# Feed-forward gate products of pairs 3 to 10 by seven half-size products (a Strassen scheme with weight and token sums) in a transformer stack on one Trainium2 core

## What is computed

```
def swiglu(h, w_gate, w_up, w_down):
    return (jax.nn.silu(h @ w_gate) * (h @ w_up)) @ w_down

h = rms_norm(x, ffn_norm[i])
x = x + swiglu(h, ffn_w_gate[i], ffn_w_up[i], ffn_w_down[i])
```

## Time and profile before

| | |
|---|---|
| median of three runs | 2059.2 us |
| the profiled execution | 2057.88 us, of which the span of instructions is 2055.9 us |
| TensorE, matmuls | busy 2024.0 us of the span (98%) |
| VectorE, ScalarE, GpSimd | busy 44%, 41%, 50% |
| first feed-forward block | pairs 3 to 10 from 258.8 to 432.9 us, the last down matmuls at 552 us |
| second feed-forward block | pairs 3 to 10 from 865.1 to 1039.2 us, the last down matmuls at 1158 us |

### The profile page before, as it was taken

The page is one execution under the profiler, slowest core; times in us unless marked ns, Lnnn a source line. Parts: engine busy times, 40 slices in busy tenths (PEclk is TensorE's granted clock), DMA queues, the critical chain, the costliest instruction groups (busy, mean ns, idle before and its releaser), DMA issues.

```text
span 2055.9 us, 25781 instructions
## 1 busy us (share of the span) xinstructions
PE 2024.0 (98%) x9884; PEld 1654.1 (80%) x9884; DVE 896.8 (44%) x1411; ACT 840.8 (41%) x1341; POOL 1032.9 (50%) x855
## 2 busy tenths in 40 slices
PE   9999999999999999999999999999999999999998
PEld 7888888888877777888888778988887876677787
DVE  3184433322144435334322388778875215443331
ACT  4123222222244443222222377677774325544543
POOL 4455544545532224544545468788885441323242
PEclk9999999999999999999999999999999999999999
DMA  5223233223433312333233334434432321112131
GB/s 169 97 87 113 83 103 103 84 84 97 126 91 93 92 42 82 103 103 102 84 89 101 102 105 123 122 104 114 133 103 62 105 84 62 60 63 81 43 103 62
DMA packets 259365, 193.28 MB, mean 94 GB/s; under 512 B 9459, under 2 KB 247335, under 8 KB 259256
## 3 DMA queue, kind: packets, MB, share of 16 engines
q1 hardware_dynamic: 256188, 190.67, 30.9%
q10 hardware_dynamic: 3068, 1.09, 0.2%
HBM read 189.46 MB, written 2.27 MB: 93 GB/s over the span
## 4 chain that ended last, share of the span: by engine, by line
PE 38%; issue 35%; POOL 21%; DVE 2%; ACT 2%; DMA 1%; POOLq 0%; SPq 0%; ACTq 0%; DVEq 0%
POOL wlo L652 21%; PE bank L2058 11%; PE bank L2060 11%; PE bank L2059 11%; PE bank L2541 1%; PE bank L2537 1%; PE bank L2505 1%; DMA raw<-in_conv_w_in 0%; DVE xc L1668 0%; ACT whi L741 0%; DVE hLo L1971 0%; DMA rows<-cums 0%; PE bank L2519 0%; PE bank L2493 0%; PE bank L2477 0%
## 5 line engine op out<-in xcount | busy, mean ns | idle before, releaser
L652 POOL TENSOR_TENSOR wlo<-raw,whi 128x512 fp32r<-128x512 f32 (+1 forms) x664 | 842.4, 1299 | 942.7 <-ACT whi L741 942.7
L2058 PE MATMUL bank<-hHi,whi 128*128 128x512 f32 (+1 forms) x1392 | 548.4, 394 | 3.8 <-DVE qk L1554 1.5
L2060 PE MATMUL bank<-hHi,wlo 128*128 128x512 f32 (+1 forms) x1392 | 540.7, 388 | 0.0
L2059 PE MATMUL bank<-hLo,whi 128*128 128x512 f32 (+1 forms) x1392 | 540.4, 388 | 0.0
L741 ACT ACTIVATE whi<-raw 128x2048 fp32r<-128x2048 f32 (+1 forms) x167 | 301.8, 1807 | 476.0 <-PE bank L2060 473.0
L2058 PEld LDWEIGHTS bank<-hHi,whi 128*128 128x128 f32 x1392 | 261.4, 188 | 63.2 <-issue 6.6
L2060 PEld LDWEIGHTS bank<-hHi,wlo 128*128 128x128 f32 x1392 | 261.3, 188 | 54.8
L2059 PEld LDWEIGHTS bank<-hLo,whi 128*128 128x128 f32 x1392 | 261.5, 188 | 53.2 <-issue 1.2
L2058 PE MATMUL bank<-whi,hHi 128*128 128x256 f32 (+1 forms) x640 | 219.4, 343 | 2.2 <-POOL wlo L652 1.8
L2060 PE MATMUL bank<-whi,hLo 128*128 128x256 f32 (+1 forms) x640 | 208.5, 326 | 0.0
L2059 PE MATMUL bank<-wlo,hHi 128*128 128x256 f32 (+1 forms) x640 | 208.3, 326 | 0.0
(11 more groups left out here) (387 smaller groups left out, 2930.7 us busy)
## 6 DMA issues: line engine op xcount, KB each, us to landing
raw<-in_ssd_w_in SPq DMA_DIRECT2D x48, 512.0 KB, 4.8
raw<-in_ffn_w_gate SPq DMA_DIRECT2D x44, 512.0 KB, 4.7
raw<-in_ffn_w_up SPq DMA_DIRECT2D x44, 512.0 KB, 4.7
raw<-in_gla_w_in SPq DMA_DIRECT2D x40, 512.0 KB, 4.6
rows<-cums SPq DMA_DIRECT2D x64, 256.0 KB, 5.4
raw<-in_ffn_w_down SPq DMA_DIRECT2D x32, 384.0 KB, 3.6
raw<-in_attn_w_qkv SPq DMA_DIRECT2D x24, 512.0 KB, 4.5
raw<-in_conv_w_in SPq DMA_DIRECT2D x23, 512.0 KB, 4.4
```

Of the source, the lines that this page charges most:

```text
L652: ins = pool.tensor_tensor(wlo[s][:, part], raw[s][:, part], whi[s][:, part].bitcast(F32), ALU.subtract)
L2058: pe.matmul(dst, hi1, hi2, start=first, stop=False)
L2059: pe.matmul(dst, hi1, lo2, start=False, stop=False)
L2060: return pe.matmul(dst, lo1, hi2, start=False, stop=last)
```

## The change

Only the feed-forward blocks change, and in them pairs 3 to 10 (eight of eleven). The gate product of such a pair is no longer one unit. The product of a weight block (1024 rows by 256 columns) and the tokens (1024 by 512) is cut in two by two quarters in the inner dimension and the columns, and inner dimension and tokens, and is made by seven products of half size in every dimension, with sums of weight quarters (`S1` to `S4`) and sums of token quarters (`T1` to `T4`). Each of the seven is 4 inner tiles by 3 matmuls of 128 x 256, 84 matmuls of 256 columns in place of 48 of 512. The up unit stays 48 matmuls of 512, in four parts of 12 (`u0` to `u3`). TensorE goes through eleven parts in the order of `TURNS`; `S2` and `S3` are added on to bank 0 after its contents were copied out (`kept`), `S4` on to bank 1 after bank 1 was read.

- **Buffers.** `whi` and `wlo` become a ring of eight quarters of 128 x 512. ScalarE rounds each quarter (`turn_high`) once TensorE is through with the part eight turns back, GpSimd makes its low part (`turn_low`). Per pair that is 11 roundings and 11 subtractions of 512 in place of 2 of 2048 and 8 of 512.
- **Added, per pair.** VectorE: the four weight sums of the next pair (512 wide, both inputs and the output in SBUF), four additions of 256 wide that put the blocks of the gate tiles together from a bank and a kept copy (`block`), two products with `rstd` in SBUF (`scaled`, in place of the two reads from the bank). ScalarE: three copies of 256 wide out of bank 0 (`kept`).
- **Added, per block.** ScalarE writes the gained input plain (8 copies, after pair 0); VectorE makes the four token sums of it (1024 wide); ScalarE rounds them in four copies of 1024, GpSimd makes their low parts in eight subtractions of 512 (before unit 5 and before the turns of pair 3).
- **Moved.** VectorE no longer writes `aHi` and `aLo` in each pair; it leaves the plain product (`plain`, which lies where `aLo` is). The 22 roundings (`act_high`, ScalarE) and 22 subtractions (`odd_low` GpSimd, `even_lows` VectorE) come in the last pair and where the down product begins, since the sums lie where `aHi` is. The down product's first output tile waits for these.
- **Waits.** Before the first part of pair 3 TensorE waits for the `a_done` of both tiles of pair 2. SyncE loads the next gate unit after the low part of `22` and the sum `S4` of the pair, the next up unit after the low part of `u3`.

The core of the diff:

```diff
+TURNS = ["11", "12", "S2", "S1", "S3", "22", "u0", "S4", "u1", "u2", "u3"]
...
+            def turn_low(j, i, name):
+                pool.wait_ge(*late("q_hi", turned_by(j, i, name)))
+                pool.tensor_tensor(v3(slot(wlo, j, i, name), 4), source(j, i, name), v3(slot(whi, j, i, name), 4).bitcast(F32),
+                                   ALU.subtract).then_inc(L("q_lo"), 1)
...
+                for t in (1, 3, 5):
+                    odd_low(j, t)
+                pool.sem_inc(w_lo, 2 * SEVENS)
+                low(u_down + 1, 0, DOWN)
+                for t in (7, 9, 11, 13, 15):
+                    odd_low(j, t)
+                low(u_down + 2, 1, DOWN)
+                for t in (17, 19, 21):
+                    odd_low(j, t)
...
+                def turn_high(i, name):
+                    r = turn_at(i, name)
+                    if r >= 8:
+                        act.wait_ge(*late("q_mm", QUARTERS * j + r - 7))
+                    else:
+                        act.wait_ge(mm, 2 * (u_up + 2 * FIRST_SEVEN - (r < 4)))
...
+                    act.activation(v3(slot(whi, j, i, name), 4), source(j, i, name), ACT.Copy).then_inc(L("q_hi"), 1)
...
+                def sevens(i):
+                    kept(i, 0, "11")
+                    turn_high(i, "u1")
+                    turn_high(i, "u2")
+                    kept(i, 1, "S2")
+                    turn_high(i, "u3")
+                    kept(i, 2, "S3")
+                    if i == FT // 2 - 1:
+                        for t in range(8):
+                            act_high(t)
+                        gate_silu(i, 0, 1)
+                        turn_down(0)
+                        gate_silu(i, 1, 0)
+                        for t in range(8, 19):
+                            act_high(t)
+                        turn_down(1)
+                        for t in range(19, FT):
+                            act_high(t)
+                        return
...
-                        chain(tt(t32[b][:, :], bank[2 + b][:, :], tile(sil, b), ALU.mult))
-                        chain(tt(t32[b][:, :], t32[b][:, :], rstd[:, :], ALU.mult))
-                        chain(dve.tensor_copy(tile(aHi, 2 * i + b), t32[b][:, :]))
-                        tt(tile(aLo, 2 * i + b), t32[b][:, :], tile(aHi, 2 * i + b).bitcast(F32), ALU.subtract).then_inc(S(f"a_done{j}"), 1)
...
+                def up(i, b, src, n):
+                    dve.wait_ge(S(f"sil_ready{j}"), 2 * i + n + 1 + 1)
+                    chain(tt(plain(j, 2 * i + b), src[:, :], tile(sil, b), ALU.mult))
+                    tt(plain(j, 2 * i + b), plain(j, 2 * i + b), rstd[:, :], ALU.mult).then_inc(S(f"a_done{j}"), 1)
...
+                def sevens(i):
+                    more = i < FT // 2 - 1
+                    block(i, 0, 0, 0, bank[2], "12")
+                    block(i, 1, 1, 2, bank[1], "S1")
+                    block(i, 1, 0, 2, bank[3], "22")
+                    if more:
+                        first_sums(i + 1)
+                    scaled(i, 1, 3)
+                    block(i, 0, 1, 1, bank[1], "S4")
+                    scaled(i, 0, 4)
+                    if more:
+                        last_sums(i + 1)
+                    else:
+                        even_lows((0, 2, 4, 6))
+                    for b in range(2):
+                        dve.wait_ge(*late("q_mm", turned_by(j, i, f"u{2 * b + 1}")))
+                        up(i, b, bank[4 + b], 1 - b)
+                        if not more and b == 0:
+                            even_lows((8, 10, 12))
...
+                def quarter(dst, i, name, moving, first, width, last=True):
+                    pe.wait_ge(*late("q_lo", turned_by(j, i, name)))
+                    hi, lo = slot(whi, j, i, name), slot(wlo, j, i, name)
+                    for n in range(4):
+                        w = slice(P * n, P * (n + 1))
+                        Hi, Lo = moving(n)
+                        to, begin = dst[:, 0:width], first and n == 0
+                        pe.matmul(to, hi[:, w], Hi, start=begin, stop=False, skip_group_check=True)
+                        pe.matmul(to, hi[:, w], Lo, start=False, stop=False, skip_group_check=True)
+                        ins = pe.matmul(to, lo[:, w], Hi, start=False, stop=last and n == 3, skip_group_check=True)
+                    ins.then_inc(L("q_mm"), 1)
...
+                    if again:
+                        pe.wait_ge(*late("kept", 3 * v))
+                    else:
+                        pe.wait_ge(S(f"gs_ready{j}"), 2 * i + 1)
+                        pe.wait_ge(S(f"a_done{j}"), 2 * i + 1)
+                    quarter(bank[0], i, "11", half(0, 0), True, 256)
+                    if again:
+                        pe.wait_ge(*late("c_made", 4 * v))
+                    quarter(bank[2], i, "12", half(1, 0), True, 256)
+                    pe.wait_ge(*late("kept", 3 * v + 1))
+                    quarter(bank[0], i, "S2", summed(i, 2, 0), False, 256)
+                    quarter(bank[1], i, "S1", summed(i, 0, 1), True, 256)
+                    pe.wait_ge(*late("kept", 3 * v + 2))
+                    quarter(bank[0], i, "S3", summed(i, 1, 2), False, 256)
+                    quarter(bank[3], i, "22", summed(i, 3, 3), True, 256)
+                    if again:
+                        pe.wait_ge(S(f"a_done{j}"), 2 * i)
+                    quarter(bank[4], i, "u0", whole(0), True, SEQ, False)
```

## The result

The changed kernel takes 2065.02 us (median of 9 runs, 2062.89 to 2066.57) against 2059.63 for the kernel before (9 runs): a ratio of 1.0028, 95% interval 1.0020 to 1.0036. It is slower by 0.28%. The forecast was 2054.0 us and faster. The profiled execution took 2064.30 us with a span of 2062.6, 6.4 us more than the one before.

A forecast was written before the change was run, and what follows sets the result against it. TensorE, busy 98% of the span, was taken as the bound. Profiled 2057.88 - 13.0 (narrower gate matmuls) + 5.0 + 2.8 (two stalls) = 2052.7, median 1.3 above: 2054.0 us; range for 8 in 10, 2048.0 to 2066.5.

The forecast's parts named there:

- The gain: Gate units in pairs 3 to 10: 84 narrow matmuls replace 48 wide ones, 0.81 us less each, 13.0 us in all.
- Borders with satisfied waits: Rival: each of 176 part borders costs TensorE even when its wait is satisfied; 0.03 us each erases the gain; chance 0.17.
- the copies out of bank 0 kept their margin: Rival: ScalarE's kept copies miss their 0.8 us margin in the pairs; 0.3 us past it costs 4.8 us; chance 0.07 with other late waits.
- Stall 1: Where pair 3 begins, TensorE waits for pair 2's last up tile: 2.5 us a block, 5.0 in all, bounds 1.8 and 2.9.
- stall 2: Where down begins, TensorE waits for GpSimd's low parts of units two and three: 1.4 us a block, bounds 0 and 2.6.
- The rival that I gave 0.10: GpSimd held up by VectorE steps with two SBUF inputs at down start: 6.2 us a block, 2066.4 us; chance 0.10.
- the forecast's own mechanism: Matmul gain less the stalls at pair 3 and down start: 2054.0 us, bounds 2049.8 to 2057.2; chance 0.58.
- The wider range: Whole-kernel time range for 8 in 10: 2048.0 to 2066.5 us.
- the first rival: At down start, GpSimd held up by VectorE steps with two SBUF inputs: 2066.4 us; chance 0.10.

The follow-up runs named there:

- e8_bank_start: Changed kernel with pair 3 waiting for each bank separately and VectorE's even-tile subtractions at down start reading one input from PSUM bank 7: 2046.75 us, 0.9943 of the kernel before.
- e3_start: Changed kernel with TensorE at pair 3 waiting for each bank by itself, not for both up tiles at the first part: 2059.49 us, 1.0005 of the kernel before.
- e1_bank_input: Changed kernel with VectorE's even-tile subtractions at down start taking one input from PSUM bank 7 (values not the product's): 2053.16 us, 0.9973 of the kernel before.
- e7_share: Changed kernel with per-bank waits at pair 3, ScalarE and GpSimd reordered at down start, tiles 19 and 21 moved to VectorE: 2048.86 us, 0.9951 of the kernel before.

## Why the prediction was wrong

**The gain was right.** 13.0 us by the two pitches: the pairs run without a gap at 0.120 and 0.227, and e8_bank_start finds 12.3 us. Borders with satisfied waits cost nothing that shows (0.4 us a block in all, against 0.03 us each in the rival), and the copies out of bank 0 kept their margin (the first of the last pair ended at 411.35, and S2 began at 412.20): both of those rivals fall. By the gap that the Trainium skill gives for isolated matmuls (TensorE: Matmul & The Clock Gate, Back-to-back issue gap) the gain would have been an estimated 19 us; the trace decides against it.

**Stall 1 was nearly right.** 2.5 us forecast, 2.05 measured with 0.07 of a longer first matmul. VectorE's product with `rstd` took 1.03 us, between my 0.69 and 1.40: it began at 259.63, when 0.44 us of a GpSimd step were left (that one's successor began at 260.07 and took 1.73). e3_start takes the stall away and gains 4.7 us, against 5.0 forecast for it.

**The step that failed is the size of stall 2**, 1.4 us a block against 4.6. The chain was the right one and began on time (the first down unit's low part at 423.14, which is 13.8 us after the last pair's start at 430.32 - 20.95, forecast 13.9). What followed was priced at 3.65 to 4.32, 6.8 and again 3.65 to 4.32 us and took 5.30, 8.55 and 5.37: 19.2 against the 14.1 to 15.4 of the bounds. The rival that I gave 0.10, GpSimd held up by VectorE, is what happened; e1_bank_input shows it, with 14.8 us for the same three groups once VectorE reads a bank. Alone the three groups would be 3.65 + 5 x 1.26 + 3.65 = 13.6 us, and 14 VectorE steps with two SBUF inputs lay beside them (eleven tiles, two products with `rstd`, one scaling; the first and the last in part), 0.40 us of GpSimd's time for each. That rival had nine steps at 0.69 us and no half clock, so its 2066.4 lies near the 2065.0 measured by luck, as its errors cancel; its mechanism was right.

I had argued against it from GpSimd's 5.48 with VectorE's steps beside it against 5.45 without. The 5.45 was not without: VectorE's fourth step, with both inputs in SBUF, began at 391.48, and more such steps lay beside other groups of the pairs. A group in the trace of before that had no VectorE step with two SBUF inputs beside it, ahead of the second block, is

```profile
788.99 5.04 POOL L652 TENSOR_TENSOR wlo<-raw,whi 128x512 fp32r<-128x512 f32 x4 [2.19 <-ACT whi L741]
```

1.26 a step, and the group just before it had taken 5.91. One VectorE step with two SBUF inputs in a group already cost GpSimd 0.4 us (5.45 against 5.04), two cost it 0.9 (5.91 in the trace of before, 7.22 against 5 x 1.26 in e1_bank_input, 4.53 against 3.65 in e7_share), and the eleven that e1_bank_input changed, in 20 us, cost it 4.4. So the price is 0.4 to 0.45 us for each such step, and the steps could have been counted.

**The half clock was not in the sum**, a term put at nothing without a reason. It cost 1.6 us at the first pair 3 and 1.7 and 2.9 at the down starts, 6.2 in the profiled execution. In the two feed-forward blocks of these traces, all four gaps of 4.6 us (the changed kernel and e3_start, two blocks each) went with a stretch at the half clock, three of ten gaps of 2.05 to 2.53 us did, and none of the gaps of 1.2 or less. Why three of the ten did and seven did not stays open. Together: stall 2 was 6.4 us too small, the clock 6.2, stall 1 0.8 too large: 2054.0 + 6.4 + 6.2 - 0.8 = 2065.8 against 2065.0.

The bounds of the forecast's own mechanism, 2049.8 to 2057.2, did not hold the time, and it went the other way than forecast. The wider range held it only because it took in the first rival.

## What to carry to other kernels

Before pricing work that goes to two engines at once, find a group of the one that had the other idle for its whole length, and one that had it busy, and count the steps of the other in it: a pair of rows that differ by 0.03 us says nothing if both have company. Where a queue takes over many small steps at a border, follow every unit that is behind them, not only the next: relieving the second showed the third. A wait of some microseconds on TensorE can be dearer than its length, since a stretch at half clock can follow; several waits of 0.2 to 0.8 us in its place cost in these traces only themselves and 0.1 us each for the start.

## What the runs showed of the hardware

- A GpSimd subtraction of 128 x 512 took 1.26 us alone, and 1.71 to 1.74 with VectorE steps with two SBUF inputs beside it throughout; VectorE's own then took 1.4 to 1.7 in place of 0.69. With one input in PSUM, VectorE took 0.62 a step and GpSimd 3.65 / 4 = 0.91 for the narrow ones with no two-input step beside them, and 7.22 / 5 = 1.44 for the wide ones with two. The Trainium skill (SBUF — State Buffer, Who interferes with whom) says that a VectorE instruction with two SBUF inputs contends with a GpSimd one that reads SBUF, and that the second to come fully blocks until the first is through. The trace agrees that either side can lose, but GpSimd lost 0.4 to 0.45 us for each VectorE step and not its full 0.69.
- In the pairs the same contention is present (GpSimd's steps beside a two-input step were 1.74) and cost nothing, as GpSimd was ahead: in the last pair its low parts of S2 and S1 ended at 405.26 and 406.96, and TensorE began them at 412.20 and 413.64.
- At the half clock (TensorE granted 1.2 GHz) the distance between 512-wide matmuls is 0.43 us in place of 0.227, and between 256-wide ones 0.21 in place of 0.120; one such stretch cost 1.6 to 2.9 us here.
